# Two modulation panels ahead of an even merge item and two between its gate and branch products

## The chip, the cores and the metric

The kernel runs on one core of a Trainium2 chip. The metric is the device time of one execution in microseconds (us), the median of several runs. The engines are named as the profile names them: PE is TensorE (matmuls; PEld its weight loads), ACT is ScalarE, DVE is VectorE, POOL is GpSimd, and SP is SyncE, which here does nothing but issue DMAs. Each engine works through its own list of instructions in order, and engines wait for each other on semaphores. An instruction that waits holds up everything behind it on its engine.

## The reference

Two blocks follow each other on 256 tokens of width 1024. The change touches the first block, which has two layers. In a layer three branches (attention, pooling, gated linear attention or GLA) are merged:

```python
gates = jax.nn.sigmoid(zz['merge'].astype(jnp.float32))
g_mla, g_pool, g_gla = jnp.split(gates, N_BRANCH, axis=-1)
merged = g_mla * (y_mla @ w_bm) + g_pool * (y_pool @ w_bp) + g_gla * (y_gla @ w_bg)
return merged @ w_out
```

Each layer also takes a modulation: `silu(c) @ mod_w + mod_b`, a vector of 3 x 1024 numbers per layer, split in shift, scale and gate. It depends on the condition `c` alone, so it can be computed at any time before it is used. The gate of layer 0 is first used behind layer 0's merge, and all three parts of layer 1 are used in layer 1.

## The kernel before, in words

**Weights.** All weights stream from memory in 328 panels of 512 KB (8 blocks of 128x128 floats). SP issues their loads in one fixed order into 6 slots: the load of panel n waits until PE has released panel n-6. PE releases a panel with its first product on the next one. A "split" panel goes through two more steps before PE may use it: ACT rounds it to `panels_hi` (line 402, four such buffers), and POOL takes the rest, `panels - panels_hi`, in two halves (lines 412 and 413). A product on a split panel is three matmuls (lines 368 to 370). The modulation's panels are not split: a product on them is one matmul (line 372, shown by the profile as two records).

**The merge of layer 0.** It has 24 items, 8 for each branch. Item i has eight gate products (128 rows of the merge logits for 512 tokens, on block column i), then four branch products. ACT takes the sigmoid of the gate (line 1268), DVE multiplies it with the branch result (line 1277) and, from item 8 on, adds it to the sum (line 1280). Between items PE, ACT and DVE do the steps of the GLA branch: scores behind items 3 and 9, chunk states behind items 4 and 10, outputs behind items 7 and 11, norm sums behind item 12, and the spread of the norm behind item 13.

**Modulation in the merge.** Four of the six rounds of modulation (the third part of layer 0 and the three of layer 1) lie in this merge. Each round is cut in two halves of 4 panels, and a half stands ahead of every even item from 2 to 16: the first half at items 2, 6, 10 and 14, the second half at items 4, 8, 12 and 16. With the second half the round is complete, and three more steps follow: ACT copies the row of results out of the PSUM bank (`mod_copy`, line 545), PE transposes it back into the same bank (`mod_turn`, line 538, at the end of the item), and DVE adds the bias (`mod_use`). `mod_turn` waits for `mod_copy`.

**Names for panels.** In this text the 7 panels between one modulated item i and the next are called, in the order of before: M0, M1, M2, M3 (modulation), G (the gate weights of item i), J0 (the branch weights of item i and half of the gate weights of item i+1) and J1 (the rest of item i+1). A prime marks those of the next modulated item: M0', M1', G'.

**What sets the order.** The order of PE is written out by hand. The order of the roundings on ACT is derived from it: `blocks.mark("gate", l, i)` notes how far PE has come in the panels at that point, and `rounding.before`, called ahead of the sigmoid of item i, places on ACT all the roundings that can be made without PE going past that point. ACT therefore waits there for the landing of each of these panels, with the sigmoid queued behind.

Of the kernel before, what the change touches and what calls it, by code (L numbers as in the profile page):

```python
# [25 lines left out]
P = 128  # L26
# [35 lines left out]
MOD_HALVES = {2: (0, 2, 0), 4: (0, 2, 1), 6: (1, 0, 0), 8: (1, 0, 1), 10: (1, 1, 0), 12: (1, 1, 1), 14: (1, 2, 0), 16: (1, 2, 1)}  # L62
# [46 lines left out]
def stream_plan():  # L109
# [10 lines left out]
    def add_round(l, n, half):  # L120
        add(f"mod{l}_{n}_{half}", [[part("mod_w", l, k * P, P, n * D + j * MOD_COLS + q * P, P)]
                                   for k in range(KD // 2 * half, KD // 2 * (half + 1)) for j in range(MOD_GROUPS)
                                   for q in range(MOD_COLS // P)])

    for n in MOD_FIRST:
        for half in range(2):
            add_round(0, n, half)
    for l in range(DEPTH):
# [115 lines left out]
def build(nc, weights, vectors, constants, x_in, c_in, out):  # L244
# [11 lines left out]
    with ctx:  # L256
# [266 lines left out]
        def mod_half(pe, i, l, n, half, bank):  # L523
            if i and half == 0:
                pe.wait_ge(mod_row if i < len(MOD_FIRST) else mod_used, i)
            for k in range(KD // 2):
                for j in range(MOD_GROUPS):
                    w = blocks.lhs(pe, plan[f"mod{l}_{n}_{half}"] + (k * MOD_GROUPS + j) * 2, (0, P), 2)
                    last = half == 1 and k == KD // 2 - 1
                    blocks.product(pe, ps[32 * j:32 * j + 32, bank, 0:MOD_COLS], silu_c[:, KD // 2 * half + k, :], w,  # L530
                                   half == 0 and k == 0, last, mod_filled if last and j == MOD_GROUPS - 1 else None)
# [96 lines left out]
        def first_modulation():  # L628

            def tensor(pe):  # L630
                for i, n in enumerate(MOD_FIRST):
                    mod_half(pe, i, 0, n, 0, 6)
                    mod_half(pe, i, 0, n, 1, 6)
# [537 lines left out]
        def gla_and_merge(l, TQ, ys, gq_at, gqkv, ga, free_at, inputs):  # L1171
# [61 lines left out]
            def items(pe, first, end):  # L1233
                for i in range(first, end):
                    if l == 0 and i in MOD_HALVES:
                        inputs.pool_banks_free(pe)
                        l2, n, half = MOD_HALVES[i]
                        mod_half(pe, mod_index(l2, n), l2, n, half, 3)
# [1499 lines left out]
```

## Time and profile before

| | us |
|---|---|
| runs: median of 3 (lowest, highest) | 1546.7 (1545.67, 1548.7) |
| span of the profiled execution, first to last instruction | 1541.0 |
| run median less that span: what lies around the span | 5.7 |
| PE busy | 1376.8 (89%) |
| DVE busy | 846.5 (55%) |
| POOL busy | 733.2 (48%) |
| ACT busy | 639.2 (41%) |

The profiled execution has no separate time of its own beside its span. PE's work is what fills the span. The merge of layer 0 with its modulation runs from about 300 to 570 us; the modulated items are 317 to 517 us. A difference within 0.2% (3 us) would not be told from no change.

### The profile page before, as it was taken

What the parts mean: (1) busy time and instruction counts of PE and PEld (TensorE: products, weight loads), DVE (VectorE), ACT (ScalarE), POOL (GpSimd) and SP (SyncE); (2) the same over time, 40 slices, a digit from 0 to 9 for tenths busy, and PEclk for the clock granted to TensorE, in tenths of its full rate; (3) what the DMA queues carried; (4) which work ended last, traced back from release to release, by engine and by line L of the source; (5) the groups of instructions that cost most, each with busy time, mean ns of one, the idle gap of its engine ahead of it and who ended that gap; (6) DMA issues with size and microseconds to landing.
All of it is one profiled execution on the core that took longest, in us unless ns stands there. A gap on an engine that the chain in (4) does not pass through costs nothing.

```text
span 1541.0 us, 24544 instructions
## 1 busy us (share of the span) xinstructions
PE 1376.8 (89%) x10288; PEld 1153.1 (75%) x10288; DVE 846.5 (55%) x1213; ACT 639.2 (41%) x1004; POOL 733.2 (48%) x512
## 2 busy tenths in 40 slices
PE   5798899999999999698899899978799888799997
PEld 1654688777777787383787789968688777799996
DVE  2567515431424340657577557479898644598801
ACT  3535322433322323446334554747421123555542
POOL 0520044323212644050696758738644204499983
PEclk8899999999989999799999999989899999999998
DMA  8320123244334432030334335525222134266552
GB/s 340 121 68 14 41 87 101 101 172 142 137 111 175 150 96 82 28 122 16 111 122 137 110 111 157 157 96 177 71 86 71 53 97 124 96 181 189 179 178 82
DMA packets 49118, 180.79 MB, mean 117 GB/s; under 512 B 5488, under 2 KB 6512, under 8 KB 48624
## 3 DMA queue, kind: packets, MB, share of 16 engines
q1 hardware_dynamic: 48864, 177.13, 35.6%
q8 instruction: 81, 1.33, 0.3%
q10 hardware_dynamic: 144, 2.10, 0.3%
q14 instruction: 29, 0.24, 0.1%
HBM read 178.16 MB, written 1.05 MB: 116 GB/s over the span
## 4 chain that ended last, share of the span: by engine, by line
PE 67%; DVE 19%; ACT 5%; DMA 4%; issue 3%; POOL 2%; SPq 0%; ACTq 0%; DVEq 0%
PE ps L368 17%; PE ps L370 16%; PE ps L369 16%; PE ps L372 16%; DMA panels<-weights 3%; DVE work L1838 2%; POOL panels_r L412 1%; ACT panels_hi L402 1%; POOL panels_r L413 1%; PE ps L959 1%; DVE work L1280 1%; DMA const_sb<-constants 1%; DVE small L1007 1%; DVE work_r L1283 1%; DVE work L802 1%
## 5 line engine op out<-in xcount | busy, mean ns | idle before, releaser
L412 POOL TENSOR_TENSOR panels_r<-panels,panels_hi 128x512 fp32r<-128x512 f32 x254 | 373.0, 1468 | 787.1 <-ACT panels_hi L402 785.7
L369 PE MATMUL ps<-h_sb_r,panels_hi 128*128 128x256 f32 (+1 forms) x1408 | 452.0, 321 | 0.0
L402 ACT ACTIVATE panels_hi<-panels 128x1024 fp32r<-128x1024 f32 x254 | 267.5, 1057 | 412.1 <-PE ps L370 236.0
L413 POOL TENSOR_TENSOR panels_r<-panels,panels_hi 128x512 fp32r<-128x512 f32 x254 | 373.4, 1470 | 0.0
L368 PE MATMUL ps<-hi_sb_r,panels_hi 128*128 128x512 f32 (+1 forms) x784 | 278.6, 355 | 27.9 <-DVE h_sb_r L683 14.0
L369 PEld LDWEIGHTS ps<-h_sb_r,panels_hi 128*128 128x128 f32 x1408 | 275.7, 196 | 17.7 <-issue 0.7
L370 PE MATMUL ps<-hi_sb_r,panels_r 128*128 128x512 f32 (+1 forms) x784 | 272.9, 348 | 0.0
L368 PE MATMUL ps<-h_sb_r,panels_hi 128*128 128x256 f32 x624 | 183.6, 294 | 12.3 <-DVE h_sb_r L664 7.6
L368 PE MATMUL ps<-work_r,panels_hi 128*128 128x256 f32 (+1 forms) x560 | 182.7, 326 | 11.7 <-POOL panels_r L413 7.6
L368 PEld LDWEIGHTS ps<-hi_sb_r,panels_hi 128*128 128x128 f32 x784 | 152.9, 195 | 53.6 <-DVE h_sb_r L683 15.3
L370 PE MATMUL ps<-h_sb_r,panels_r 128*128 128x256 f32 x624 | 178.9, 287 | 0.0
L370 PE MATMUL ps<-work_r,panels_r 128*128 128x256 f32 (+1 forms) x560 | 175.5, 313 | 0.0
L369 PE MATMUL ps<-work_r,panels_hi 128*128 128x256 f32 (+1 forms) x560 | 175.5, 313 | 0.0
L370 PEld LDWEIGHTS ps<-hi_sb_r,panels_r 128*128 128x128 f32 x784 | 152.4, 194 | 18.0
L368 PEld LDWEIGHTS ps<-h_sb_r,panels_hi 128*128 128x128 f32 x624 | 122.2, 196 | 16.9 <-DVE h_sb_r L664 8.8
L368 PEld LDWEIGHTS ps<-work_r,panels_hi 128*128 128x128 f32 x560 | 106.5, 190 | 23.8 <-POOL panels_r L413 6.9
L372 PE MATMUL ps<-work 64*64 64x64 f32 (+7 forms) x1496 | 110.6, 273 | 14.2 <-DVE work L1441 5.9
L370 PEld LDWEIGHTS ps<-h_sb_r,panels_r 128*128 128x128 f32 x624 | 122.5, 196 | 0.0
L369 PEld LDWEIGHTS ps<-work_r,panels_hi 128*128 128x128 f32 x560 | 106.4, 190 | 7.8 <-issue 1.4
L370 PEld LDWEIGHTS ps<-work_r,panels_r 128*128 128x128 f32 x560 | 106.4, 190 | 6.4
L372 PEld LDWEIGHTS ps<-work 64*64 64x64 f32 (+4 forms) x1496 | 71.9, 142 | 42.7 <-issue 18.1
L372 PE MATMUL ps<-work,panels 128*128 128x256 f32 (+2 forms) x288 | 87.9, 463 | 13.7 <-DVE work L2267 5.7
(325 smaller groups left out, 1814.7 us busy)
## 6 DMA issues: line engine op xcount, KB each, us to landing
panels<-weights SPq DMA_DIRECT2D x328, 512.0 KB, 3.6
x_sb<-x_in SPq DMA_DIRECT2D x1, 2048.0 KB, 8.5
x_sb<-x_in ACTq DMA_DIRECT2D x1, 2048.0 KB, 9.6
const_sb<-constants SPq DMA_DIRECT2D x1, 1216.0 KB, 11.0
out<-x_sb SPq DMA_DIRECT2D x2, 512.0 KB, 3.1
vec_sb<-vectors SPq DMA_DIRECT2D x1, 725.0 KB, 12.3
small<-c_in SPq DMA_DIRECT2D x1, 8.0 KB, 1.8
```

The lines of the kernel that those rows point to most:

```text
L368: pe.matmul(o, lhsT.hi, rhs.hi, start=start, stop=False)
L369: pe.matmul(o, lhsT.hi, rhs.lo, start=False, stop=False)
L370: mm = pe.matmul(o, lhsT.lo, rhs.hi, start=False, stop=stop)
L372: mm = pe.matmul(o, lhsT, rhs, start=start, stop=stop)
L402: act.activation(panels_hi[:, m:m + PANEL * P], panels[:, n:n + PANEL * P], ACT.Copy).then_inc(panel_rounded, 1)
L412: pool.tensor_tensor(panels_r[:, at:at + half], panels[:, at:at + half], panels_hi[:, m:m + half], ALU.subtract)
L413: pool.tensor_tensor(panels_r[:, at + half:at + 2 * half], panels[:, at + half:at + 2 * half], panels_hi[:, m + half:m + 2 * half], ALU.su ...
L802: steps["dve"](dve.reciprocal(inverse, root))
L959: mm = pe.transpose(ps[:, 4 + kt // (nkt // 2), (kt % (nkt // 2)) * 256 + t * P: (kt % (nkt // 2)) * 256 + (t + 1) * P], probs[j % 3][:, t ...
L1007: step(dve.tensor_reduce(share[:, i % 3, :], ps[:, 2 * (i % 2):2 * (i % 2) + 2, 0:nk], AX.X, ALU.max))
L1280: dve.tensor_tensor(merged[:, m, :], merged[:, m, :], dst, ALU.add).then_inc(added, 1)
L1838: ins = dve.tensor_tensor_scan(x_c[:, part, i, :], mag[:, i:i + 1].to_broadcast([P, T]), x_c[:, part, i, :], 0.0, ALU.mult, ALU.add)
```

## The change

The modulation is counted in four parts of 2 panels for each round instead of two halves of 4. At an even item from 2 to 16 one part stays ahead of the gate products, and the other goes behind the gate products and ahead of the branch products. To let the weights follow that order, the branch weights of an item get their own entry in the plan (`join{l}_{i}`). The number of panels and of products is the same. The mark `"gate"`, from which the roundings are placed, now stands behind the second part. On ACT `mod_copy` moves from ahead of the roundings of its item to behind the sigmoid of its item.

```diff
-MOD_HALVES = {2: (0, 2, 0), 4: (0, 2, 1), 6: (1, 0, 0), 8: (1, 0, 1), ...}
+MOD_PARTS = 4
+MOD_LATER = ((0, 2), (1, 0), (1, 1), (1, 2))
+MOD_ITEMS = {2 + 4 * r + 2 * half: (l, n, half) for r, (l, n) in enumerate(MOD_LATER) for half in range(2)}
...
-            if l == 0 and i in MOD_HALVES:
-                add_round(*MOD_HALVES[i])
-            add(f"merge{l}_{i}", tiles_of("w_in", l, D, IN_AT["merge"] + b * D + m * P, P)
-                + tiles_of(("w_branch_mla", "w_branch_pool", "w_branch_gla")[b], l, 512, m * P, P), split=True)
+            with_mod = l == 0 and i in MOD_ITEMS
+            if with_mod:
+                l2, n, half = MOD_ITEMS[i]
+                add_part(l2, n, 2 * half)
+            add(f"merge{l}_{i}", tiles_of("w_in", l, D, IN_AT["merge"] + b * D + m * P, P), split=True)
+            if with_mod:
+                add_part(l2, n, 2 * half + 1)
+            add(f"join{l}_{i}", tiles_of(("w_branch_mla", "w_branch_pool", "w_branch_gla")[b], l, 512, m * P, P), split=True)
...
 def items(pe, first, end):
-                    if l == 0 and i in MOD_HALVES:
+                    with_mod = l == 0 and i in MOD_ITEMS
+                    if with_mod:
                         inputs.pool_banks_free(pe)
-                        mod_half(pe, mod_index(l2, n), l2, n, half, 3)
+                        mod_part(pe, mod_index(l2, n), l2, n, 2 * half, 3)
...
                     for k in range(KD):
                         blocks.product(pe, ps[:, gate, 0:TQ], blocks.lhs(pe, at + k), ...)
+                    if with_mod:
+                        mod_part(pe, mod_index(l2, n), l2, n, 2 * half + 1, 3)
                     blocks.mark("gate", l, i)
...
-                        blocks.product(pe, ps[:, branch, 0:TQ], blocks.lhs(pe, at + KD + k), parts[b][:, k, :], ...)
-                    if l == 0 and i in MOD_HALVES and MOD_HALVES[i][2] == 1:
-                        mod_turn(pe, mod_index(*MOD_HALVES[i][:2]), 3)
+                        blocks.product(pe, ps[:, branch, 0:TQ], blocks.lhs(pe, plan[f"join{l}_{i}"] + k), parts[b][:, k, :], ...)
+                    if with_mod and half == 1:
+                        mod_turn(pe, mod_index(l2, n), 3)
...
 def gates(act, first, end):
                 for i in range(first, end):
-                    if l == 0 and i in MOD_HALVES and MOD_HALVES[i][2] == 1:
-                        mod_copy(act, mod_index(*MOD_HALVES[i][:2]), 3)
                     rounding.before(act, "gate", l, i)
...
                     act.activation(sig[:, i % 2, :], ps[:, 4 + 2 * (i % 2), 0:TQ], ACT.Sigmoid).then_inc(gated, 1)
+                    if l == 0 and i in MOD_ITEMS and MOD_ITEMS[i][2] == 1:
+                        mod_copy(act, mod_index(*MOD_ITEMS[i][:2]), 3)
```

The built order of ACT before, around item 4 (between the key copies behind item 3 and the sigmoid of item 5); each row's wait stands behind it, and `panel_loaded5` and `panel_loaded0` are the landings of J0 and J1:

```order
L1396 ACTIVATE work<-ps 128x512 [waits gla_k_turned] x2
L545 ACTIVATE small<-ps 128x256 [waits mod_turned,mod_filled]
L402 ACTIVATE panels_hi<-panels 128x1024 [waits panel_used,panel_loaded5]
L402 ACTIVATE panels_hi<-panels 128x1024 [waits panel_used,panel_loaded0]
L1268 ACTIVATE work<-ps 128x512 [waits merge_mixed,merge_filled]
L1450 ACTIVATE x_sb<-work,small 128x128 [waits gla_kv_taken] x14
L402 ACTIVATE panels_hi<-panels 128x1024 [waits panel_used,panel_loaded5]
L1268 ACTIVATE work<-ps 128x512 [waits merge_mixed,merge_filled]
```

The same place on ACT after the change; line 409 is the rounding, 1277 the sigmoid, 553 `mod_copy`, 1461 the carried states, and `panel_loaded3` is the landing of G', the gate panel of item 6:

```order
L1407 ACTIVATE work<-ps 128x512 [waits gla_k_turned] x2
L409 ACTIVATE panels_hi<-panels 128x1024 [waits panel_used,panel_loaded5]
L409 ACTIVATE panels_hi<-panels 128x1024 [waits panel_used,panel_loaded0]
L409 ACTIVATE panels_hi<-panels 128x1024 [waits panel_used,panel_loaded3]
L1277 ACTIVATE work<-ps 128x512 [waits merge_mixed,merge_filled]
L553 ACTIVATE small<-ps 128x256 [waits mod_turned,mod_filled]
L1461 ACTIVATE x_sb<-work,small 128x128 [waits gla_kv_taken] x14
L1277 ACTIVATE work<-ps 128x512 [waits merge_mixed,merge_filled]
```

The rounding of G' moved from the sigmoid of the odd item to ahead of the sigmoid of the even one, and `mod_copy` moved behind both. Items 8 and 12 read the same; at item 8 a table load (`ACT_TABLE_LOAD`) stands between the third rounding and the sigmoid. At item 16 four roundings stand there.

The built order of PE before, in item 4, from its last modulation panel to the transposes (between the rows with dots stand the other gate and branch products):

```order
L372 MATMUL ps<-panels,small 32x256 [waits panel_loaded2]
L372 MATMUL ps<-panels,small 32x256 x3
L372 MATMUL ps<-panels,small 32x256 [waits panel_loaded3]
L368 MATMUL ps<-hi_sb_r,panels_hi 128x512 [waits panel_split,merge_mixed]
...
L368 MATMUL ps<-work_r,panels_hi 128x512 [waits panel_split]
...
L538 MATMUL ps<-const_sb,small 128x128 [waits mod_used,mod_row]
```

And after the change, where line 379 is a modulation product, 375 the first matmul of a split product and 546 the transposes:

```order
L375 MATMUL ps<-hi_sb_r,panels_hi 128x512 [waits panel_split,merge_mixed]
...
L379 MATMUL ps<-panels,small 32x256 [waits panel_loaded3]
L379 MATMUL ps<-panels,small 32x256 x3
L379 MATMUL ps<-panels,small 32x256 [waits panel_loaded4]
L375 MATMUL ps<-work_r,panels_hi 128x512 [waits panel_split]
...
L546 MATMUL ps<-const_sb,small 128x128 [waits mod_used,mod_row]
```

Two of the four panels moved behind the gate products; the transposes, with their wait for `mod_copy` (`mod_row`), stay at the end of the item. The orders of DVE, POOL and SP are unchanged.

## Rows read from the trace of the kernel before

**Rows 1.** The page: the chain that ended last, by engine.

```profile
PE 67%; DVE 19%; ACT 5%; DMA 4%; issue 3%; POOL 2%; SPq 0%; ACTq 0%; DVEq 0%
```

**Rows 2.** Waits, 300 to 530 us: waiter, releaser, us in total, times, longest.

```profile
PE ps L368 <- POOL panels_r L413: 9.4, 9, 3.1
```

**Rows 3.** Timeline of PE, item 4: start, us, instruction, [idle before <-releaser].

```profile
339.31 1.93 PE L372 MATMUL ps<-panels,small 128*32 128x256 f32 x32
...
341.18 0.50 PE L368 MATMUL ps<-hi_sb_r,panels_hi 128*128 128x512 f32 x1
...
348.41 0.50 PE L368 MATMUL ps<-work_r,panels_hi 128*128 128x512 f32 x1 [1.50 <-POOL panels_r L413]
...
351.27 0.38 PE L538 MATMUL ps<-const_sb,small 128*128 128x128 f32 x2
...
355.00 0.65 PE L372 MATMUL ps<-work 64*64 64x128 f32 x8 [1.46 <-DVE work L1441]
```

**Rows 4.** Timeline of ACT: items 4, 8 and 12.

```profile
344.71 1.06 ACT L402 ACTIVATE panels_hi<-panels 128x1024 fp32r<-128x1024 f32 x1 [2.98 <-DMA panels<-weights]
...
345.98 1.06 ACT L402 ACTIVATE panels_hi<-panels 128x1024 fp32r<-128x1024 f32 x1 [0.21 <-DMA panels<-weights]
...
346.95 0.60 ACT L1268 ACTIVATE work<-ps 128x512 f32<-128x512 f32 x1
...
402.16 1.28 ACT L1268 ACT_TABLE_LOAD   x1
...
465.91 1.06 ACT L402 ACTIVATE panels_hi<-panels 128x1024 fp32r<-128x1024 f32 x1 [4.67 <-DMA panels<-weights]
```

**Rows 5.** Chain, 300 to 530 us: start, us from issue to landing, what.

```profile
317.64 4.49 DMA panels<-weights
...
339.96 4.72 DMA panels<-weights
...
359.33 3.47 DMA panels<-weights
```

**Rows 6.** Timeline of PE: items 2, 6, 8, 10, 12, 13 and 16.

```profile
326.00 0.50 PE L368 MATMUL ps<-work_r,panels_hi 128*128 128x512 f32 x1 [0.47 <-POOL panels_r L413]
...
366.61 0.47 PE L368 MATMUL ps<-hi_sb_r,panels_hi 128*128 128x512 f32 x1 [0.69 <-POOL panels_r L413]
...
393.16 1.07 PE L372 MATMUL ps<-panels,small 128*32 128x256 f32 x16
...
406.72 0.38 PE L538 MATMUL ps<-const_sb,small 128*128 128x128 f32 x2
...
417.39 1.48 PE L372 MATMUL ps<-panels,small 128*32 128x256 f32 x21
...
431.76 0.65 PE L372 MATMUL ps<-work 64*64 64x128 f32 x8 [1.56 <-DVE work L1441]
...
466.79 0.38 PE L538 MATMUL ps<-const_sb,small 128*128 128x128 f32 x2
...
484.55 1.12 PE L372 MATMUL ps<-work,const_sb 128*128 128x512 f32 x2 [1.40 <-DVE work L1529]
...
504.64 1.93 PE L372 MATMUL ps<-panels,small 128*32 128x256 f32 x32
...
507.94 0.47 PE L368 MATMUL ps<-hi_sb_r,panels_hi 128*128 128x512 f32 x1 [1.36 <-POOL panels_r L413]
...
516.20 0.38 PE L538 MATMUL ps<-const_sb,small 128*128 128x128 f32 x2
```

**Rows 7.** Timeline of DVE, item 10.

```profile
428.34 0.69 DVE L1277 TENSOR_TENSOR work<-ps,work 128x512 f32<-128x512 f32 x1 [7.14 <-PE ps L370]
```

**Rows 8.** Windows: stretch, length, busy by engine, PEclk, DMA share, GB/s.

```profile
400.00:407.00 7.00, 3.85 (x19) 2.88 (x18) 0.08 (x1) 4.03 (x5) 4.99 (x4) 1.00 0.41 137
...
427.00:437.00 10.00, 8.44 (x75) 6.56 (x74) 5.04 (x16) 4.20 (x14) 0.72 (x1) 0.83 0.20 54
...
525.00:560.00 35.00, 35.00 (x156) 28.97 (x156) 16.15 (x20) 9.82 (x11) 16.80 (x13) 1.00 0.32 94
```

More of the change, by code:

```diff
@@ L118, in add, with add_part @@
         split_panels.extend([split] * (-(-len(order) // PANEL) - len(split_panels)))
[L120 to L123, printed above, removed]
+    def add_part(l, n, part_of_round):
+        ks = KD // MOD_PARTS
+        add(f"mod{l}_{n}_{part_of_round}", [[part("mod_w", l, k * P, P, n * D + j * MOD_COLS + q * P, P)]
+                                            for k in range(ks * part_of_round, ks * (part_of_round + 1)) for j in range(MOD_GROUPS)
+                                            for q in range(MOD_COLS // P)])
     for n in MOD_FIRST:
-        for half in range(2):
-            add_round(0, n, half)
+        for a in range(MOD_PARTS):
+            add_part(0, n, a)
     for l in range(DEPTH):
@@ L521, in build, with mod_part @@
         row_sb = region(small, 512, MOD_COLS)
-        def mod_half(pe, i, l, n, half, bank):
-            if i and half == 0:
+        def mod_part(pe, i, l, n, a, bank):
+            ks = KD // MOD_PARTS
+            if i and a == 0:
                 pe.wait_ge(mod_row if i < len(MOD_FIRST) else mod_used, i)
-            for k in range(KD // 2):
+            for k in range(ks):
                 for j in range(MOD_GROUPS):
[L528 to L531, printed above, removed]
+                    w = blocks.lhs(pe, plan[f"mod{l}_{n}_{a}"] + (k * MOD_GROUPS + j) * 2, (0, P), 2)
+                    last = a == MOD_PARTS - 1 and k == ks - 1
+                    blocks.product(pe, ps[32 * j:32 * j + 32, bank, 0:MOD_COLS], silu_c[:, ks * a + k, :], w,
+                                   a == 0 and k == 0, last, mod_filled if last and j == MOD_GROUPS - 1 else None)
         def mod_turn(pe, i, bank):
@@ L631, in tensor @@
                 for i, n in enumerate(MOD_FIRST):
-                    mod_half(pe, i, 0, n, 0, 6)
-                    mod_half(pe, i, 0, n, 1, 6)
+                    for a in range(MOD_PARTS):
+                        mod_part(pe, i, 0, n, a, 6)
                     mod_turn(pe, i, 7)
@@ L1252, in items @@
                     for k in range(4):
[L1253 removed]
+                        blocks.product(pe, ps[:, branch, 0:TQ], blocks.lhs(pe, plan[f"join{l}_{i}"] + k), parts[b][:, k, :], k == 0, k == 3,
                                        filled if k == 3 else None)
[L1255 to L1256 removed]
+                    if with_mod and half == 1:
+                        mod_turn(pe, mod_index(l2, n), 3)
             def gates(act, first, end):
                 for i in range(first, end):
[L1260 to L1261 removed]
                     rounding.before(act, "gate", l, i)
@@ L1285, in mixes @@
                                           ALU.subtract).then_inc(merged_ready[0], 1)
-                    if l == 0 and i in MOD_HALVES and MOD_HALVES[i][2] == 1:
-                        l2, n, _ = MOD_HALVES[i]
+                    if l == 0 and i in MOD_ITEMS and MOD_ITEMS[i][2] == 1:
+                        l2, n, _ = MOD_ITEMS[i]
                         mod_use(dve, mod_index(l2, n), l2, n, 3)
```

4 lines of the change are left out of this document (1 added, 3 removed).

## The prediction

> **What bounds the kernel now.** I read the page's chain first: 67% of it is PE [rows 1], so a microsecond of wait on PE in the chain is a microsecond of time. Behind the merge nothing absorbs a delay: from 525 to 560 us PE is busy 35.0 of 35.0 us [rows 8]. Then the waits of the stretch of the change: PE waited 9.4 us in nine waits for POOL's half of a rounded panel [rows 2]. That is all that a smoother flow of panels could win.
>
> The timeline of PE shows one modulated item in full. In item 4 the four modulation panels start at 339.31, the gate products at 341.18 and the first branch product at 348.41, after 1.50 of wait; the transposes start at 351.27 [rows 3]. So four modulation panels take 1.87, the gate products 348.41 - 1.50 - 341.18 = 5.73, the branch products with the step behind them 2.86. The wait of 1.50 is J0's. Its load was issued at 339.96, 0.65 after M0 began (the first product on M0 releases J1), and took 4.72 [rows 5]; ACT began to round it at 344.71 [rows 4]. Most other waits are J0's too; G's are those at 366.61 and 507.94 [rows 6].
>
> **What the change removes.** G' moves forward: its slot is free once M3 begins, 11 us before G' is used. G's waits go (0.69 and 1.36 [rows 6]). But PE meets J0 at the same distance behind M0 as before: ahead of it stand the same four panels and the same gate products, only in another order, and J0's load still waits for the first product on M0. Items 2, 6, 10 and 14 thus keep their time from M0 to J0. In item 2 J0 began after a wait at 326.00, load issued at 317.64 [rows 5, 6]; both stay. At item 6 the 0.69 is taken back by J0: its weights are ready 0.65 + 3.47 + 3.70 = 7.8 after M0 at the earliest (issue, shortest landing, and 348.41 - 344.71 for both halves of the rounding), while PE comes there at 1.87 + 5.73 = 7.6. I take 0 for these four, and keep a gain of up to 2 us as the low end. Twice more per item PE changes between kinds of matmul. The first matmul behind a change took 0.50 against some 0.39 of others; eight items by two by 0.11 is 1.8 at most, and it falls where PE then waits for J0, so I take 0. Parts of 2 panels in the first modulation, ahead of everything, keep the same order: 0.
>
> **What the change adds.** At items 4, 8, 12 and 16 PE's transposes at the end of the item wait for `mod_copy`. Before, that stood ahead of J0's rounding and was long done. Now it stands behind three roundings and the sigmoid, and the third rounding waits for the landing of G'. Behind the waiting transposes PE has everything else. Timetable from the start of M0, all from item 4:
>
> - M2 starts at 1.87/2 + 5.73 = 6.67.
> - Its first product releases G: SP issues M1' at 6.67 + 0.65 = 7.32. G' is issued half a microsecond later, so it follows M1' by one transfer.
> - M1' lands after 3.47, the shortest row [rows 5], at 10.79. Landings of loads in flight together are 345.98 - 344.71 = 1.27 apart [rows 4]: G' lands at 12.06.
> - ACT: 346.95 - 345.98 = 0.97 for the rounding, 0.60 for the sigmoid [rows 4], and for the copy, half its columns, between 0.3 and 0.6; I take 0.4. Together 1.97, so the transposes start at 14.03.
>
> In item 4 they started at 351.27 - 339.31 = 11.96. **Item 4: +2.1.**
>
> **Item 8.** M0 starts at 393.16 and the transposes at 406.72 [rows 6]. G' lands at 405.22, and behind its rounding comes the table load of 1.28 [rows 4]: 405.22 + 1.97 + 1.28 = 408.5. **+1.8.**
>
> **Item 12.** Here the input `x` (2 MB) loads on ACT's queue at the same time. In the rows J1's rounding waited for its landing until 465.91 [rows 4]. M0', M1' and G' are the next three in the queue: 465.9 + 3 x 1.27 = 469.7, plus 1.97 is 471.7, against 466.79 [rows 6]. **+4.9.** If `x` no longer delayed them, the timetable alone would give +2.0.
>
> **Item 16.** Four roundings; the fourth panel's load is issued when M2 starts to work, 504.64 + 7.32 = 511.96, and lands alone after 3.5: 515.4, plus 1.97 is 517.4, against 516.20 [rows 6], which had the 1.36 of G in it. **+1.2.**
>
> **Item 10** has no transposes, but its sigmoid is late in the same way, and DVE's product behind it precedes the summing of chunk states, for which PE waits in its chunk-state step. G' lands at 417.39 + 12.06 = 429.45; rounding and sigmoid end at 431.0; DVE's product began at 428.34 [rows 6, 7]. The wait of 1.56 at 431.76 [rows 6] grows. **+2.7.** At items 2, 6 and 14 the late sigmoid costs nothing: it ends 12.06 + 0.97 + 0.60 = 13.6 after M0, and the next to need its bank are the gate products of item i+2, at 7.6 + 2.86 + 5.73 + 2.86 + 0.94 = 20.0.
>
> **Item 13** gains. Its sigmoid waited on ACT for G of item 14; now that rounding lies behind it, so DVE comes in time and the 1.40 at 484.55 [rows 6] goes. **-1.4.**
>
> Sum without the clock: 2.1 + 1.8 + 4.9 + 1.2 + 2.7 - 1.4 = +11.3.
>
> **The clock.** From 427 to 437 PE's granted clock was 0.83 [rows 8]: 3.4 us of ten at the lower level (1.2 GHz), around a wait of 1.56 between small matmuls. From 400 to 407, around the longest panel wait (3.1 [rows 2]) between long matmuls, it stayed at 1.00. A stretch of 3.4 us at half speed costs dense work 1.7. The change makes waits of 2 to 5 us on PE at five places. I take two more low stretches, +3.4; the ends are 0 and five, 8.5.
>
> The Trainium skill ("TensorE: Matmul & The Clock Gate", section "HAM oscillation — how this bites in real kernels") says that a PE which stands waiting for a DMA goes back to the low clock, each time anew. By that rule all five waits would pay. The row at 400 to 407 did not follow it, so it is a rival and not the forecast. The skill's "DMA: Bandwidth & Descriptors" (section "Anatomy of one DMA — SWDGE (gpsimd) path") fits a transfer as 2.0 us plus its bytes at 436 GB/s: 3.2 us for a panel, where the rows show 3.47 to 4.72; by the page the sum would be about 1 us less.
>
> Total: 11.3 + 3.4 = +14.7. The span of 1541.0 becomes 1555.7; with the 5.7 around it, or from the median of 1546.7, the time is **1561.4 us**. Each term is a difference within one execution and carries over to the median as it stands.
>
> **Rivals.**
>
> A, every wait starts a low stretch: as a mechanism, PE leaves each of the five waits at 1.2 GHz for 3.4 us of long matmuls. 11.3 + 8.5 = 19.8, so 1566.5. For it: the drop at 427 to 437. Against it: none at 400 to 407. Chance 0.10.
>
> B, not slower: the panels flow more evenly and the copies come in time. For that G' would have to land by 11.96 - 1.97 = 10.0 after M0 starts, not at 12.06; two transfers in 2.7 us instead of 4.74. Then G's waits (0.69, 1.36 and up to the rest of the 9.4 that isn't J0's, some 3 in all) and item 13's 1.4 are won: 1546.7 - 4.4 = 1542.3. Against it: no load in the rows landed in under 3.47. Chance 0.04.
>
> C, no change: the wait for the copy is real but PE gets it back later. The 35.0 of 35.0 speaks against it. 1546.7; chance 0.03.
>
> D, only the two long ones hold: G' lands so much sooner, with fewer loads in flight beside it, that items 4, 8 and 16 lose about 1 each, item 12 only its 2.0, and no low stretch is added: 3 + 2.0 + 2.7 - 1.4 = 6.3, so 1553.0. Chance 0.10.
>
> The forecast has the remaining 0.73.
>
> **Numbers.** The forecast's own ends are 11.3 without a stretch (1558.0) less 3 for faster landings, and 11.3 with three stretches (1563.1) plus 3 for later landings such as the 4.72. I give 1555 to 1566.5, which holds nearly all of the forecast's chance and half of A. A measurement tells 0.2% (3 us) from no change: faster 0.04, within it 0.04, slower 0.92.
>
> **What the profile of after would show.** Right: PE idle ahead of the transposes of items 4, 8, 12 and 16, released by ACT's copy, about 2 to 5 us each and longest at item 12; three roundings on ACT ahead of an even sigmoid, the third waiting for DMA for some 5 us; DVE's product of item 10 waiting for ACT, and a wait of over 4 us in the chunk states behind it; no wait for G, and J0's as before; no wait at item 13. Wrong: transposes that start without a wait (then B), a clock of 1.00 throughout (then 1558), or J0's waits gone, which would lower the sum by up to 6.

## The result, and the profile after

| | us |
|---|---|
| changed kernel, median of 4 runs (lowest, highest) | 1561.2 (1559.27, 1567.61) |
| before, median of 4 runs on the same chip (lowest, highest) | 1546.18 (1543.43, 1548.7) |
| ratio of the runs, 95% interval | 1.0119 [1.0097, 1.014] |
| span of the profiled execution, after (before) | 1565.8 (1541.0) |

The forecast was 1561.4 us. The ratio speaks for some 18 us more than before, 15 to 22 by its interval; the forecast added 14.7. The two medians by themselves differ by 15.0 us, a ratio of 1.0097, at the low end of that interval. A second set of runs, `changed_again` below, gave 1.0112 by its ratio and 1.0125 by its medians, so the cost is best taken as 15 to 19 us. The profiled execution of after is the longest of its four (1567.61), so its own difference, 24.8 us of span, is larger; that of `changed_again` had a span of 1560.9.

The page's chain is still PE's (compare [rows 1]):

```profile
PE 68%; DVE 18%; ACT 5%; DMA 4%; issue 3%; POOL 1%; SPq 0%; ACTq 0%; DVEq 0%
```

The waits of PE, 300 to 550 us, after (waiter, releaser, us in total, times, longest), to hold against [rows 2]:

```profile
PE ps L546 <- ACT small L553: 12.6, 4, 6.8
...
PE ps L379 <- DVE work L1452: 6.1, 2, 5.4
...
PE ps L375 <- POOL panels_r L420: 4.8, 7, 2.7
```

The same view of before, where the rows named by the prediction left these two out:

```profile
PE ps L372 <- DVE work L1441: 3.0, 2, 1.6
PE ps L372 <- DVE work L1529: 1.4, 1, 1.4
```

The first row of after is new: the transposes (line 546) wait for ACT's copy (line 553). The wait of the chunk states for DVE doubled, from 3.0 to 6.1. The waits for POOL's half of a panel fell from 9.4 [rows 2] to 4.8, and the norm's wait of 1.4 is gone. Together 12.6 + 3.1 - 4.6 - 1.4 = +9.7 us of waiting.

PE after, at the places of [rows 3] and [rows 6] (start, us, instruction, [idle before <-releaser]):

```profile
338.72 1.07 PE L379 MATMUL ps<-panels,small 128*32 128x256 f32 x16
...
345.38 1.07 PE L379 MATMUL ps<-panels,small 128*32 128x256 f32 x16
346.69 0.50 PE L375 MATMUL ps<-work_r,panels_hi 128*128 128x512 f32 x1 [0.24 <-POOL panels_r L420]
...
352.85 0.69 PE L546 MATMUL ps<-const_sb,small 128*128 128x128 f32 x2 [3.14 <-ACT small L553]
...
413.80 0.44 PE L546 MATMUL ps<-const_sb,small 128*128 128x128 f32 x2 [0.90 <-ACT small L553]
...
442.89 0.90 PE L379 MATMUL ps<-work 64*64 64x128 f32 x6 [5.43 <-DVE work L1452]
...
482.04 0.69 PE L546 MATMUL ps<-const_sb,small 128*128 128x128 f32 x2 [6.82 <-ACT small L553]
...
500.34 1.45 PE L379 MATMUL ps<-work,const_sb 128*128 128x512 f32 x3
...
536.08 0.44 PE L546 MATMUL ps<-const_sb,small 128*128 128x128 f32 x2 [1.78 <-ACT small L553]
```

M0 of item 4 starts at 338.72 and M2 at 345.38, 6.66 later (forecast 6.67). The transposes start 14.13 after M0 (forecast 14.03). The row at 500.34 is the norm's spread in item 13, now without a wait.

ACT after, items 4, 8 and 12, to hold against [rows 4]:

```profile
342.97 1.06 ACT L409 ACTIVATE panels_hi<-panels 128x1024 fp32r<-128x1024 f32 x1 [3.54 <-DMA panels<-weights]
345.48 1.06 ACT L409 ACTIVATE panels_hi<-panels 128x1024 fp32r<-128x1024 f32 x1 [1.46 <-DMA panels<-weights]
350.98 1.06 ACT L409 ACTIVATE panels_hi<-panels 128x1024 fp32r<-128x1024 f32 x1 [4.44 <-DMA panels<-weights]
351.94 0.58 ACT L1277 ACTIVATE work<-ps 128x512 f32<-128x512 f32 x1
352.42 0.38 ACT L553 ACTIVATE small<-ps 128x256 f32<-128x256 f32 x1
...
410.51 1.06 ACT L409 ACTIVATE panels_hi<-panels 128x1024 fp32r<-128x1024 f32 x1 [3.68 <-DMA panels<-weights]
411.58 1.28 ACT L1277 ACT_TABLE_LOAD   x1
...
476.36 1.06 ACT L409 ACTIVATE panels_hi<-panels 128x1024 fp32r<-128x1024 f32 x1 [6.83 <-DMA panels<-weights]
480.17 1.06 ACT L409 ACTIVATE panels_hi<-panels 128x1024 fp32r<-128x1024 f32 x1 [2.76 <-DMA panels<-weights]
```

This is the mechanism in one view. The third rounding sits 4.44 us in front of the landing of G', with the sigmoid and the copy queued behind; G' landed 350.98 - 338.72 = 12.26 after M0 (forecast 12.06), and the copy took 0.38 (forecast 0.4).

DVE after, item 10, to hold against [rows 7]:

```profile
438.37 0.69 DVE L1288 TENSOR_TENSOR work<-ps,work 128x512 f32<-128x512 f32 x1 [11.27 <-ACT work L1277]
439.09 1.80 DVE L1291 TENSOR_TENSOR work<-work 128x512 f32<-128x512 f32 x1
440.81 0.47 DVE L1449 COPY work<-ps 128x128 f32<-128x128 f32 x2
```

The product of item 10 waits for ACT as forecast. The add behind it took 1.80 us, 1.1 more than in before, where it was this row of the same view:

```profile
429.06 0.69 DVE L1280 TENSOR_TENSOR work<-work 128x512 f32<-128x512 f32 x1
```

The windows of after (stretch, length, busy of PE, PEld, DVE, ACT and POOL, PEclk, DMA share, GB/s): first the whole stretch from M0 of item 2 to the transposes of item 16, then two of its low stretches, then behind the merge:

```profile
317.60:536.10 218.50, 193.38 (x1276) 147.15 (x1275) 60.48 (x103) 64.25 (x92) 59.91 (x48) 0.91 0.41 142
351.90:362.20 10.30, 8.73 (x66) 6.99 (x67) 5.46 (x20) 5.20 (x17) 2.49 (x2) 0.50 0.01 4
...
478.20:495.30 17.10, 13.26 (x48) 11.94 (x49) 5.49 (x9) 4.66 (x6) 4.26 (x4) 0.50 0.07 27
545.00:580.00 35.00, 35.00 (x156) 29.00 (x155) 16.16 (x20) 9.82 (x11) 16.87 (x13) 1.00 0.32 97
```

And the first of them in before:

```profile
317.00:516.20 199.20, 183.84 (x1275) 141.86 (x1275) 60.16 (x102) 65.96 (x96) 60.92 (x49) 0.97 0.44 154
```

So the merge stretch grew by 218.5 - 199.2 = 19.3 us. PE's idle time in it grew from 15.4 to 25.1 (+9.8, which the waits above account for), and the same matmuls took 193.4 instead of 183.8 us (+9.5). Most of this is the clock, which was granted at 0.91 instead of 0.97: between 300 and 600 us it was at the lower level for 37.5 us (four stretches) instead of 13.6 (three). PE was busy for 29.6 us of the first and all of the second, so at half speed the clock makes up some (29.6 - 13.6) / 2 = 8 us, an estimate. The other 1.6 us are the price of the split itself; `early_mark` below shows it without the clock. Behind the merge PE is as dense as before ([rows 8] had 35.00 of 35.00), so nothing was given back. The remaining 24.8 - 19.3 = 5.5 us of this execution's span lie outside the stretch. There PE was busy 1198.0 us against 1193.0 in before, with 121.6 us of lower clock against 114.9; in `changed_again` it was 1193.4, so this part doesn't repeat and is not the change's.

### The profile page after: what moved, and what is told of

It reads as the page before. It is cut to its first block, busy times and chain, and to the rows that moved or that the text cites. A ratio compares the mean times of both kernels' runs of the same rounds, so it can differ in the third digit from the quotient of the medians.

```text
span 1565.8 us, 24544 instructions
## 1 busy us (share of the span) xinstructions
PE 1391.4 (89%) x10288; PEld 1161.3 (74%) x10288; DVE 846.2 (54%) x1213; ACT 640.3 (41%) x1004; POOL 731.4 (47%) x512
## 4 chain that ended last, share of the span: by engine, by line
PE 68%; DVE 18%; ACT 5%; DMA 4%; issue 3%; POOL 1%; SPq 0%; ACTq 0%; DVEq 0%
PE ps L375 17%; PE ps L379 17%; PE ps L376 17%; PE ps L377 16%; DMA panels<-weights 3%; DVE work L1849 2%; POOL panels_r L419 1%; PE ps L967 1%; DVE work L1291 1%; ACT panels_hi L409 1%; DMA const_sb<-constants 1%; DVE small L1015 1%; DVE work_r L1294 1%; DVE work L810 1%; POOL panels_r L420 1%
## 5 line engine op out<-in xcount | busy, mean ns | idle before, releaser
L376 PEld LDWEIGHTS ps<-h_sb_r,panels_hi 128*128 128x128 f32 x1408 | 276.8, 197 | 17.9 <-issue 0.7
L375 PE MATMUL ps<-work_r,panels_hi 128*128 128x256 f32 (+1 forms) x560 | 183.4, 328 | 10.2 <-POOL panels_r L420 5.9
L379 PE MATMUL ps<-work 64*64 64x64 f32 (+7 forms) x1496 | 116.3, 282 | 16.2 <-DVE work L1452 9.0
L379 PEld LDWEIGHTS ps<-work 64*64 64x64 f32 (+4 forms) x1496 | 75.2, 147 | 47.0 <-issue 19.8
L1288 DVE TENSOR_TENSOR work<-ps,work 128x512 f32<-128x512 f32 x24 | 16.6, 692 | 165.9 <-ACT work L1277 96.7
## 6 DMA issues: line engine op xcount, KB each, us to landing
x_sb<-x_in ACTq DMA_DIRECT2D x1, 2048.0 KB, 10.2
```

What stands on the lines that cost most here:

```text
L375: pe.matmul(o, lhsT.hi, rhs.hi, start=start, stop=False)
L376: pe.matmul(o, lhsT.hi, rhs.lo, start=False, stop=False)
L379: mm = pe.matmul(o, lhsT, rhs, start=start, stop=stop)
L1288: dve.tensor_tensor(dst, ps[:, 5 + 2 * (i % 2), 0:TQ], sig[:, i % 2, :], ALU.mult).then_inc(mixed, 1)
```

## The experiments

All kernels are changes to the changed kernel, except one that says otherwise. Ratios are against the kernel before, run beside them. "Low clock" is the time between 300 and 600 us of the profiled execution at which PE was granted the lower level (1.2 GHz).

### The mark back ahead of the second part

```diff
+                    blocks.mark("gate", l, i)
                     if with_mod:
                         mod_part(pe, mod_index(l2, n), l2, n, 2 * half + 1, 3)
-                    blocks.mark("gate", l, i)
```

> The mark from which the roundings are placed goes back to right behind the gate products, ahead of the second modulation part; all else is as in the changed kernel. ACT then rounds only J0 and J1 ahead of an even sigmoid, and G' ahead of the odd one. My theory (copy and sigmoid of an even item are held by the landing of G'): the waits of PE ahead of the transposes of items 4, 8 and 16 (3.14, 0.90, 1.78 us in the changed kernel's profile) fall to under 0.3, that of item 12 falls from 6.82 to 2 to 3 (J1 itself lands late beside the load of x), the chunk-state wait behind item 10 falls from 5.43 to about 1.6: 1546 to 1549 us. Rival (the split of the modulation around the gate products costs by itself, by more changes between kinds of matmul and by J0): the time stays within 4 us of 1561.

Measured: 1544.18 us, ratio 1.001 [0.9989, 1.0032]. No loss is shown any more (the interval leaves room for 0.3%), with the panels still in the new order. ACT of this kernel, item 4:

```profile
344.04 1.06 ACT L409 ACTIVATE panels_hi<-panels 128x1024 fp32r<-128x1024 f32 x1 [3.87 <-DMA panels<-weights]
346.63 1.06 ACT L409 ACTIVATE panels_hi<-panels 128x1024 fp32r<-128x1024 f32 x1 [1.54 <-DMA panels<-weights]
347.60 0.58 ACT L1277 ACTIVATE work<-ps 128x512 f32<-128x512 f32 x1
348.07 0.38 ACT L553 ACTIVATE small<-ps 128x256 f32<-128x256 f32 x1
```

Two roundings stand ahead of the sigmoid, and the copy is done 2.2 us before PE's transposes at 350.61. Only item 12 keeps a wait for the copy, 1.51. The chunk states of item 10 wait 1.57, as in before [rows 6], DVE's add there takes 0.69, and low clock is 13.6 us, as in before. The one line, a mark behind two panels instead of ahead of them, is the cause of the loss; the move of `mod_copy` behind the sigmoid costs something at item 12 alone.

The window of this kernel over the same work, from M0 of item 2 to the transposes of item 16, also shows what the split costs by itself:

```profile
318.10:515.60 197.50, 185.50 (x1276) 141.71 (x1276) 58.80 (x102) 63.34 (x93) 61.58 (x47) 0.97 0.44 155
```

PE is idle for 12.0 us instead of 15.4 in before. But it is busy for 185.5 instead of 183.8, with the same 13.6 us of low clock. So the split costs some 1.7 us of PE's own time and takes back half of what the shorter waits won.

### The transposes and the use one item later

```diff
-                    if with_mod and half == 1:
-                        mod_turn(pe, mod_index(l2, n), 3)
+                    if l == 0 and i - 1 in MOD_ITEMS and MOD_ITEMS[i - 1][2] == 1:
+                        mod_turn(pe, mod_index(*MOD_ITEMS[i - 1][:2]), 3)
...
-                    if l == 0 and i in MOD_ITEMS and MOD_ITEMS[i][2] == 1:
-                        l2, n, _ = MOD_ITEMS[i]
+                    if l == 0 and i - 1 in MOD_ITEMS and MOD_ITEMS[i - 1][2] == 1:
+                        l2, n, _ = MOD_ITEMS[i - 1]
                         mod_use(dve, mod_index(l2, n), l2, n, 3)
```

> As the changed kernel, but PE's transposes and DVE's use of the modulation row stand one item later (behind the gate products' and branch products' work of item i+1), so that nothing on PE waits for the copy at the end of item i. Theory: the four transposes' waits (12.6 us in sum in the profile) go, item 10's 5.43 stays: 1561 less 10 to 12.6, so 1549 to 1551. Rival (low clock is the cause and the waits only its sign): the waits go and the time falls by no more than 4 us.

Measured: 1551.01 us, ratio 1.0064 [1.0034, 1.0094]. No wait for the copy is left, low clock 20.5 us, and about half of the loss remains: the late sigmoid's other path. Waits of PE in this kernel, 300 to 550 us:

```profile
PE ps L379 <- DVE work L1452: 9.2, 2, 5.6
PE ps L375 <- POOL panels_r L420: 5.3, 8, 2.7
```

The chunk states wait 3.61 us at item 4 and 5.59 at item 10 (1.46 and 1.56 in before, [rows 3, 6]). The one at item 4 was hidden in the changed kernel, because the transposes ahead of it had already waited 3.14.

### The early mark at the first halves only

```diff
+                    if not (with_mod and half):
+                        blocks.mark("gate", l, i)
                     if with_mod:
                         mod_part(pe, mod_index(l2, n), l2, n, 2 * half + 1, 3)
-                    blocks.mark("gate", l, i)
+                        if half:
+                            blocks.mark("gate", l, i)
```

> The early mark only at items 2, 6, 10 and 14 (first half of a round, no copy behind the sigmoid); items 4, 8, 12 and 16 as in the changed kernel. Theory: of these four only item 10 was paid for, through DVE's product and the chunk states: its wait of 5.43 falls to about 1.6, 2.7 to 3.9 us are won, 1557 to 1558.5. Rival (late sigmoids cost at all even items): 5 us or more are won. Rival 2 (item 10's wait is covered): the time does not move.

Measured: 1556.0 us, ratio 1.0084 [1.0058, 1.0109]. The transposes wait 3.47, 0.74, 5.12 and 1.18, the chunk states of item 10 their 1.57; low clock 23.9 us. The complement of the run before it: item 10 repaired, the copies not. Against the changed kernel's 1.0112 (below) it is 0.3% less, within which the intervals overlap.

### The input loaded later

`x` (2 MB, on ACT's queue) is issued behind the gates of item 19 instead of in item 12.

```diff
             def squares(act):
...
-                if l == 0:
-                    load_x(act)
...
-                gates(act, GATES[l][2], 3 * KD)
+                gates(act, GATES[l][2], 20)
+                if l == 0:
+                    load_x(act)
+                gates(act, 20, 3 * KD)
```

> As the changed kernel, but the 2 MB load of x is issued on ACT's queue behind the sigmoid of item 19 instead of behind the squares at item 12. Theory: at item 12 G' lands 12.1 us after M0 starts instead of some 16, so the wait ahead of its transposes falls from 6.82 to 2 to 3: about 4 us less, 1557. Rival (item 12's wait is not from the transfer of x): the wait stays over 5 and the time within 2 us of 1561.

Measured: 1558.45 us, ratio 1.0101 [1.0078, 1.0124]. The transposes of item 12 wait 3.37 instead of 6.82 and 6.20. The third rounding there and the start of M2:

```profile
474.51 1.07 PE L379 MATMUL ps<-panels,small 128*32 128x256 f32 x16
480.06 1.06 ACT L409 ACTIVATE panels_hi<-panels 128x1024 fp32r<-128x1024 f32 x1 [5.91 <-DMA panels<-weights]
```

G' lands 5.55 after M2 begins, as at item 4 (5.60); with `x` in the way it was 9.35 (480.17 - 470.82) and, in `changed_again`, 8.77. So `x` held the three panels back by 3.2 to 3.8 us. From M0 to the transposes it is 16.1 us, though, against 17.9 and 17.3: a low stretch from 460.0 to 470.2 made PE come to M2 2.0 later, and that part of the wait is hidden and not won. Those of item 8 wait 2.12 (0.90 and 0.68), item 10's chunk states 5.29, and low clock is 30.7 us, so little shows in the time.

### The changed kernel once more

> The changed kernel once more, beside the others of this call. Its first profile spent 37.7 us of the stretch from 300 to 600 us at PE's lower clock, against 13.6 in before, and its execution was the longest of four. If low clock follows from the waits in every execution: 20 to 40 us again in that stretch, ratio 1.009 to 1.012. If the first profile was an outlier: under 18 us and a span near 1557.

Measured: 1562.36 us, ratio 1.0112 [1.0083, 1.0142]; waits for the copy 3.35, 0.68, 6.20 and 1.58, item 10 4.91, low clock 30.7. The waits repeat within some 0.6 us. The low clock does not repeat so well (37.5 and 30.7), which is why terms of it are told in rough numbers here.

### Work in the place of the waits

```diff
+            def fill(pe, i, n):
+                pe.wait_ge(mixed, m0 + i)
+                for _ in range(n):
+                    pe.matmul(ps[:, 4 + 2 * ((i + 1) % 2), 0:256], const("ident"), const("rope")[:, 0:256], start=True, stop=True)
...
                     if with_mod and half == 1:
+                        if i in (4, 12):
+                            fill(pe, i, 6 if i == 4 else 13)
                         mod_turn(pe, mod_index(l2, n), 3)
...
                     if i == 5:
+                        if l == 0 and d == 1:
+                            fill(pe, 10, 9)
                         pe.wait_ge(kv_taken, kv0 + 14 * d + 8)
```

> The changed kernel with matmuls that nobody reads put into PE's long waits: 6 ahead of the transposes of item 4, 13 ahead of those of item 12, 9 ahead of the chunk-state wait behind item 10 (128x256 float32, about 0.43 us each at the higher clock), each run shorter than the wait it stands in. Theory (idle PE in the waits brings the lower clock): the waits shrink by what is filled and end at the same moment, the low clock between 300 and 600 us falls from some 38 us to under 20, and the time falls by 2 to 6 us though work was added. Rival (the lower clock has another cause, or the fill isn't enough activity): low clock as before, time within 2 us of the changed kernel or longer.

Measured: 1560.89 us, ratio 1.0113 [1.0084, 1.0143]. PE of this kernel at item 12, the filling in full:

```profile
475.44 5.77 PE L1244 MATMUL ps<-const_sb 128*128 128x256 f32 x26
481.05 0.38 PE L546 MATMUL ps<-const_sb,small 128*128 128x128 f32 x2
```

The wait of 6 us is work now. Low clock was 27.3 us, in four stretches at 358, 406, 457 and 484, and the time is the same. The first three begin behind or at other waits (1.60 of the chunk states, 2.71 for J0, 0.87 of the carried states); for the one at 484.3, 2.9 us behind the filled place, none is seen. So filling a wait with this kind of work bought nothing, and this run taken alone speaks against waits as the cause of the low stretches. Whether the kind of filling matters was not tried.

### Mark and input together, and J0 of item 8

The first is the early mark with the late input. The second adds this, so that item 8's J0 is rounded ahead of the exponentials on ACT:

```diff
                 gates(act, cut[2], GATES[l][1])
+                if l == 0:
+                    rounding.before(act, "gate", l, 8, most=1)
                 exponentials(act, 1)
```

> The early mark at all items, and the load of x behind item 19. Theory: the 1.51 us wait at item 12's transposes, which the early mark left, goes, as J1 no longer shares the queues with x: 1 to 2 us below the early mark alone, ratio to before 0.998 to 1.001. Rival: the wait stays, or x now comes late for the next norm and costs 2 us or more there.

Measured: 1540.5 us, ratio 0.9981 [0.9964, 0.9999]. Item 12's wait for the copy is gone; low clock 10.2 us.

> As the last one, and at item 8 ACT rounds J0 ahead of the three exponentials of the second GLA direction. In every profile so far PE waited 2.7 to 3.2 us there for J0, whose panel had landed 2.5 us before ACT took it. Theory: that wait falls to 0.3 to 0.6, 2 us are won beyond the last kernel: ratio to before 0.996 to 0.999. Rival: the exponentials, 0.6 to 1 us later, hold the copy or the scores behind item 9 and give it back.

Measured: 1540.52 us, ratio 0.9968 [0.9949, 0.9986]. Item 8's J0 waits 0.42 instead of 2.71, but the transposes there 1.01; low clock is 10.2 us again. Against the kernel without it no difference is shown.

### The copy ahead of the roundings again

```diff
                 for i in range(first, end):
+                    if l == 0 and i in MOD_ITEMS and MOD_ITEMS[i][2] == 1:
+                        mod_copy(act, mod_index(*MOD_ITEMS[i][:2]), 3)
                     rounding.before(act, "gate", l, i)
...
-                    if l == 0 and i in MOD_ITEMS and MOD_ITEMS[i][2] == 1:
-                        mod_copy(act, mod_index(*MOD_ITEMS[i][:2]), 3)
```

> The changed kernel with the mark where the change put it (three roundings ahead of an even sigmoid), but the copy of the modulation row stands ahead of the roundings again, as in before. The two edits of ACT's order are told apart. Theory: no wait ahead of the transposes, but the copy now waits for M3's products behind the gate products, and J0's rounding waits behind the copy: J0 is ready 11.9 us after M0 starts, where PE comes at 7.6, so PE waits about 4 us for J0 at items 4, 12 and 16 (2.7 at item 8 before, now about 4 too), and item 10 keeps its 5. Ratio 1.008 to 1.012, the loss has only moved. Rival (the late place of the copy alone was the fault): ratio 0.999 to 1.002.

Measured: 1560.68 us, ratio 1.0124 [1.0103, 1.0146]. Waits of PE in this kernel, 300 to 550 us:

```profile
PE ps L375 <- POOL panels_r L420: 18.4, 8, 4.1
PE ps L379 <- DVE work L1452: 6.5, 2, 5.0
```

Low clock was 27.3 us. The other order fares no better. The copy now waits for the last modulation product, J0's rounding stands behind it, and PE waits 4.04 to 4.14 us for J0 at each of the four items instead of for the copy. So with the late mark the copy has no good place: ahead of the roundings it holds J0, behind them G' holds it. With the early mark the copy ahead of the roundings would wait for the same products; that was not tried.

### The kernel before with the two other edits

The late input and J0 of item 8 first, as above, put into the kernel before.

> The kernel before, with two edits of the last kernel: the load of x behind item 19, and J0 of item 8 rounded ahead of the exponentials. Modulation in halves of four panels as in before. If the split of the modulation has no worth of its own: item 8's J0 wait of 3.15 falls to some 0.5, item 13's 1.40 stays, ratio 0.997 to 1.000. If the gain of the last kernel is the split's (G's waits at items 2, 6, 16 and item 13's 1.40): ratio 0.9995 to 1.001, and those waits stand in the profile.

Measured: 1541.44 us, ratio 0.9987 [0.9965, 1.0009]. G's waits (0.60, 0.66, 1.32) and item 13's 1.44 are all there; low clock is 6.8 us. The two edits alone are not told from no change.

### The best version

Early mark, late input, J0 of item 8 first, and the transposes one item later.

> The last call's best kernel (early mark, x late, J0 of item 8 first) with the transposes and the use of the row one item later. In its profile only item 8's transposes waited, 1.01 us. Theory: that wait goes, up to 1 us is won, ratio to before 0.995 to 0.998. Rival: the steps cost the same wherever they stand and nothing is won.

Measured: 1537.57 us, ratio 0.9966 [0.995, 0.9982]; low clock 6.8. It beats the kernel before by 0.3% and the changed one by 1.5%. Its waits of PE, 300 to 550 us:

```profile
PE ps L375 <- POOL panels_r L420: 3.0, 7, 0.7
PE ps L379 <- DVE work L1452: 3.0, 2, 1.6
```

The panels' waits are 3.0 instead of 9.4 [rows 2]. Of these 6.4, 1.7 belong to the two other edits, which brought them to 7.7 in `before_x_late_j0_first`. The other 4.7 and item 13's 1.4 are what the new order of panels was able to win in waits, less the 1.7 that the split costs. In the time this isn't shown: 0.9966 against 0.9987 for the two edits alone, and the intervals overlap. Nor is a gain from the late transposes (0.9968 without them).

### Held waits in a kernel without them

To `early_mark_x_late`, 16 copies that the real one overwrites, ahead of it at items 4, 8, 12 and 16:

```diff
                     if l == 0 and i in MOD_ITEMS and MOD_ITEMS[i][2] == 1:
+                        act.wait_ge(mod_turned, mod_index(*MOD_ITEMS[i][:2]))
+                        for _ in range(16):
+                            steps["act"](act.activation(row_sb, const("rope")[:, 0:MOD_COLS], ACT.Copy))
                         mod_copy(act, mod_index(*MOD_ITEMS[i][:2]), 3)
```

> The version with the early mark and the late load of x has no wait of note for the copy. Here 16 further copies of 128x256 (values that the real copy then overwrites) stand on ACT ahead of the copy at items 4, 8, 12 and 16, some 0.42 us each with their steps, 6.7 us, of which 1 to 2 lie in the room that the copy had: PE's transposes should wait about 4 to 6 us at each of the four items, 16 to 24 in all, between dense matmuls and with nothing else changed in what PE does. Theory (waits of this length bring PE down to the lower clock afterwards): against that version, low clock between 300 and 600 us goes from 10.2 to over 25 us, each stretch beginning in or within some ten us behind a held wait, and the time rises by the waits and half the added low clock, 20 + 8 = +28 us, 1568. Rival (low stretches have another cause, the same waits cost only themselves): low clock stays under 14 us and the time rises by the waits alone, about +20, 1560.

Measured: 1573.24 us, ratio 1.0194 [1.0142, 1.0246]. PE at the four places:

```profile
355.08 0.69 PE L546 MATMUL ps<-const_sb,small 128*128 128x128 f32 x2 [4.79 <-ACT small L553]
...
416.41 0.69 PE L546 MATMUL ps<-const_sb,small 128*128 128x128 f32 x2 [3.08 <-ACT small L553]
...
483.58 0.44 PE L546 MATMUL ps<-const_sb,small 128*128 128x128 f32 x2 [4.16 <-ACT small L553]
...
539.26 0.69 PE L546 MATMUL ps<-const_sb,small 128*128 128x128 f32 x2 [4.79 <-ACT small L553]
```

And the windows of this kernel from the end of each wait:

```profile
354.90:358.30 3.40, 3.22 (x42) 2.90 (x44) 0.94 (x7) 0.20 (x2) 0.00 (x0) 0.50 0.01 2
416.30:419.70 3.40, 3.29 (x9) 2.71 (x10) 2.53 (x6) 1.00 (x2) 2.32 (x2) 0.50 0.00 0
484.60:494.80 10.20, 10.20 (x38) 9.14 (x39) 2.58 (x3) 2.73 (x4) 3.45 (x2) 0.50 0.00 0
539.20:542.60 3.40, 3.34 (x9) 2.76 (x10) 1.51 (x5) 0.95 (x2) 2.37 (x2) 0.50 0.00 0
```

Low clock went from 10.2 to 37.5 us. Each held wait is followed by a low stretch, three at once and one after a microsecond. Three more, 17.1 us together, stand near waits that were there already; one of them lasted 10.2 us and began 1.3 behind a wait of 0.87. The ratio rose by 0.0213, some 33 us, for 16.8 us of added waits; half of the added low clock, 13.6, makes up most of the rest (30.4 together). The two ratios come from different sets of runs, and by their intervals the rise is 24 to 42 us: an added wait of 3 to 5 us cost one and a half to two and a half times its length here. The rival that these waits cost only themselves falls. That an idle PE alone brings the clock down isn't shown: `fill` speaks against it, and the 64 copies added here are also more work on ACT, which was not told apart.

## Why the prediction was right, point by point

**What bounds, and what is not given back: right.** PE is the chain in both, and behind the merge it is busy 35.00 of 35.00 in both.

**What the change removes: right in kind, small in size.** Of the 4.6 us that the panels' waits lost (9.4 to 4.8), 3.0 are G's (0.91 at item 2, 0.69 and 1.36) and the other 1.6 J0's; item 4's went from 1.50 to 0.24, item 8's only from 3.15 to 2.70. Where such a wait lies ahead of transposes that wait anyway, it is no gain. I had taken 0 and kept 2 as the low end.

**The split's own cost: put at nothing, and wrong.** The prediction reckoned 1.8 us at most for more changes between kinds of matmul and took 0, as it would fall where PE then waits for J0. `early_mark` has before's low clock and is busy 1.7 us longer in the same stretch. So the bound was the price, and it stays.

**The timetable: right.** From M0 to the transposes, before and after, and the difference forecast:

| | before | after | measured | forecast |
|---|---|---|---|---|
| item 4 | 11.96 | 14.13 | +2.2 | +2.1 |
| item 8 | 13.56 | 15.69 | +2.1 | +1.8 |
| item 12 | 12.28 | 17.90 | +5.6 | +4.9 |
| item 16 | 11.56 | 12.83 | +1.3 | +1.2 |
| item 10, M0 to the end of the chunk states' wait | 14.37 | 18.36 | +4.0 | +2.7 |
| item 13 | 1.40 | 0 | -1.4 | -1.4 |

The sum is +13.8 against 11.3. `early_mark` shows the cause of all but item 13: with two roundings ahead of the sigmoid they are gone together, but for 0.3 at item 12. At item 8 the wait reads 0.90 only, since a low stretch (409.9 to 413.4) slowed PE's matmuls while ACT was late anyway: what is behind a fixed timetable doesn't pay for the clock. Item 12's share of `x` is the 3.2 to 3.8 us of `x_late`; I had 4.9 - 2.0 = 2.9.

**Item 10: the mechanism right, the size 1.3 short.** DVE's product came 2.9 later (13.84 after M0 instead of 10.95), near the 2.7. The rest is the add behind it, 1.80 instead of 0.69, which I had taken at the duration it had before. Late by 2.9, it starts beside POOL's subtraction of the third panel. This row of POOL began just ahead of it:

```profile
439.08 1.26 POOL L420 TENSOR_TENSOR panels_r<-panels,panels_hi 128x512 fp32r<-128x512 f32 x1
```

The Trainium skill, "SBUF — State Buffer", section "Terms", has DVE and GpSimd share a pair of ports that one of them holds for its whole instruction, while the other is blocked. The trace agrees: POOL's instruction ends at 440.34, and the add ends 0.55 later, 1.1 us longer than alone. The product at 438.37, which reads one input from PSUM, kept its 0.69 beside POOL's first half.

**Missed: the chunk states of item 4.** The prediction named item 10 alone. `late_turn` showed 3.61 at item 4 too. It cost nothing here (its wait even fell from 1.46 to 0.62), since the transposes had waited first; in a sum of terms it was hidden by another term, by luck.

**The clock: right in sign, too small.** Forecast: two more stretches of 3.4 us, each costing 1.7, +3.4. In the profile there was one stretch more and not two, four instead of three, but they were 10.2, 3.4, 6.8 and 17.1 us long. The matmuls took 9.5 us longer (7.2 in `changed_again`), of which some 1.7 are the split's. The length of a stretch, taken at 3.4, was the term that was mis-sized: the clock cost 5.5 to 8 us, not 3.4. Of these microseconds some lie under the waits, as at item 8. Rival A had every wait start a low stretch. In after three of the five did, those of 3.14, 5.43 and 6.82 us; the fourth stretch begins 1.3 us behind J0's wait of 2.70 at item 8, where before had none behind 3.15. So rival A's mechanism held for the long waits, at a higher price than its 1.7 each.

**How the sum came out.** In the profile: items +13.8, G's and J0's in the first halves -1.3, the chunk states of item 4 -0.8, which leaves 19.3 - 11.7 = 7.6 for the clock and the rest of the split's cost. In `changed_again` the stretch grew by 216.2 - 199.2 = 17.0. By the ratios, 1.0119 and 1.0112, the change costs 17 to 18 us, so the 14.7 was some 3 short. That the time was met to 0.2 us is luck: it rests on the medians of that one set of runs, and the terms were off one against the other, item 10, the clock and the split too small, the gains at the panels taken at nothing.

**Rivals.** B is refuted by the waits; what it had hoped for is real (5.9 instead of 9.4 us of panel waits in `early_mark`, and no wait at item 13), but only with the mark where ACT is not made to wait. C and D fell with the time.

## What to carry to other kernels

When a look-ahead (here, which roundings may go ahead of an instruction) is derived from a mark in another engine's program, moving the mark past two more panels puts a wait for a far later transfer ahead of everything behind it. Count what is queued behind the waiting instruction and who waits for each of those. And where two paths are late together, taking one away shows the other: price each alone.

## What the runs showed of the hardware

**Waits and the granted clock.** In seven kernels of this study (after, `changed_again`, `x_late`, `late_turn`, `early_mark_first_halves`, `copy_first`, `held_copy`) PE had 15 waits of 4 us and more (4.04 to 6.82) between 300 and 600 us. Every one had a low stretch, which began between 3.8 us before the wait's end and 1.0 behind it. Of the eight waits between 3.0 and 3.7 us, before's among them, six had one that began within 2 us of their end. The wait of 2.7 us for J0 of item 8, the same in nine of the kernels, had one within 2 us at six of them and none at `early_mark` and `early_mark_x_late`; at `x_late` one began only behind the next wait, of 2.12. Of the 29 waits of 1.3 to 1.8 us in all the kernels nine had one within 2 us. All nine are among the 17 at the chunk states, behind a run of 64x128 matmuls. So the length of the wait is not the whole of it. The Trainium skill ("TensorE: Matmul & The Clock Gate", section "HAM oscillation — how this bites in real kernels") says that a PE that stands waiting falls back each time; the waits of 4 us and more agree, and the shorter ones only in part. Open are why a wait of 6 us filled with matmuls did not save its stretch, and what sets a stretch's length (3.4 to 17.1 us).

**DVE beside POOL.** The 128x512 add with both inputs in SBUF took 0.69 us alone and 1.79 to 1.81 where it started 0.01 to 0.03 behind POOL's subtraction: in before at 416.43, 443.49 and 468.28, and at item 10 in after, `changed_again`, `x_late`, `late_turn`, `fill` and `copy_first`. Where POOL was 0.32 ahead (533.70 in before) it took 1.52. With the early mark, where it starts clear of POOL, it took 0.69 at item 10. Where the add is first it is POOL that pays, 1.80 us instead of 1.27, as here in before, ahead of G's wait of 1.36 at item 16:

```profile
505.98 0.69 DVE L1280 TENSOR_TENSOR work<-work 128x512 f32<-128x512 f32 x1
505.99 1.80 POOL L413 TENSOR_TENSOR panels_r<-panels,panels_hi 128x512 fp32r<-128x512 f32 x1
```
